# First projection block of a two-layer encoder step: the norm weight loaded as one row and spread by TensorE, the first weight unit and the first norm in halves, both full token tiles loaded ahead of it, low parts made in the order in which TensorE reads them

## The chip, the cores and the metric

The kernel runs on one core of one Trainium2 chip. The metric is the device time of one execution in microseconds (us), of which a run gives several; the median counts. The engines are TensorE (PE in the profile; its weight loads are PEld), VectorE (DVE), ScalarE (ACT), GpSimd (POOL) and SyncE (SP), which here only issues transfers.

## What is computed

One inference step for 256 new frames and 64 continued frames through two layers, each an attention sub-layer and a mixture of 16 experts. The change touches only the beginning of layer 0: the first norm and the first block of columns of the projection.

```python
def rms_norm(x, gain):
    xf = x.astype(jnp.float32)
    y = xf * lax.rsqrt(jnp.mean(xf * xf, axis=-1, keepdims=True) + EPS)
    return (y * gain.astype(jnp.float32)).astype(x.dtype)
...
        hp = rms_norm(xp, norm_mix[i])
        hs = rms_norm(xs, norm_mix[i])
...
    q, k, v = jnp.split(h @ w_in, 3, axis=-1)     # layer 0: w_in is 1024 x 3072, float32
```

`x` has 1024 columns, and everything is float32.

## The kernel before

**Tiles and units.** The tokens are three tiles of 128 rows (`x[:, t, :]`, t = 0, 1, 2); the third has 64 real rows. The weights of a projection come in units of 1 MB: 512 rows by 512 columns, kept as 128 partitions of four blocks of 512 numbers (`w_raw`, six slots). A block `b` of 512 output columns needs two units, `half` 0 (input rows 0 to 511) and `half` 1 (rows 512 to 1023). Layer 0 has six such blocks (q, q, k, k, v, v), then attention, the output projection and the experts, and layer 1 follows with the same stages.

**Split products.** To keep float32 accuracy, every weight and every activation of a projection is split in two: a high part that ScalarE makes by a copy to the rounded type (`split_hi` L769 for weights into `w_hi`, `h_high` L797 for activations into `hT_hi`), and a low part, the difference, that VectorE makes (`split_lo` L1680 into `w_lo`, `h_low` L1702 into `hT_lo`). TensorE then does three matmuls of 128x512 per 128 input rows, high by high, high by low and low by high (L1114 to L1116). For tile 2 the low rows lie in the unused partitions of `hT_hi`, and two matmuls are enough (L1169, L1170). One `half` of a block is therefore 12 + 12 + 8 = 32 matmuls.

**The first block.** SyncE issues, in this order, `x` tile 0, the identity, the norm weight spread over 128 partitions by the transfer (512 KB), unit 0, `x` tile 1, unit 1, `x` tile 2, the other constants, and further units as their slots become free. For each tile ScalarE squares and sums (L791), GpSimd makes the reciprocal root (L601, L602), VectorE multiplies by it and by the norm weight (L1692), TensorE transposes eight blocks of 128x128 into the memory banks of `ps` (L1141), ScalarE and VectorE make high and low parts. TensorE transposes tile 0 first, does the first six matmuls of tile 0, transposes tile 1, does the next twelve, transposes tile 2, and goes on; from there the work of `half` 1, and of all blocks behind it, follows without transposes of `h`.

**Order.** Each engine has its instructions in program order, written out by hand, and waits on counting semaphores: `lo_ready` counts units whose low part is there, `lo0` the low parts of `hT`, `h_ready0` the normed tiles, `hi_ready` the high parts of units. In ScalarE's order the high part of unit 0 stands ahead of the copies of tile 0's transposes, and the high part of unit 1 ahead of the square of tile 2. In VectorE's order the low part of unit 0 stands ahead of tile 0's low parts and of tile 1's norm.

Slots of weights are released by TensorE's progress (`units_used`), so SyncE issues most later transfers when TensorE has finished with an earlier unit.

Elsewhere in the kernel `stay_busy(bank, n)` (L1118 to L1122) issues n matmuls of 128x256 on constants whose result nobody reads.

## Time and profile before

| what | value |
|---|---|
| time of the kernel before, median of 3 runs | 958.04 us |
| the three runs | 958.04, 959.68, 950.64 us |
| the profiled execution: its own time | 956.53 us |
| its span (first to last instruction) | 954.7 us |
| TensorE busy, share of the span | 96% |
| VectorE, ScalarE, GpSimd busy | 42%, 32%, 17% |
| mean granted clock of TensorE | 0.987 |

The span is what the profile's rows are counted in; 1.8 us of the execution's time lie around it. A row of the timeline has start and duration in us, the engine, the line, the operation with output and inputs, how many instructions it stands for, and in square brackets how long the engine had been idle and what ended that. A full-precision matmul (L1122, or L1206 of the changed kernel) shows as two records in the trace, a split product's matmul and a transpose as one.

### The profile page before, as it was taken

The numbers are of one execution on the slowest core, as the hardware profiler recorded it, in microseconds if no ns is written. First come the engines' busy times: TensorE is split into PE (matmuls) and PEld (weight loads), VectorE is DVE, ScalarE is ACT, GpSimd is POOL, SyncE is SP. The second block draws the span as 40 slices with busy tenths as digits, with TensorE's granted clock in tenths as the row PEclk, the third lists the DMA queues.
The fourth block names the chain that finished last, engine by engine and source line by source line (L and its number), as shares of the span: only waits on it lengthen the run. The fifth ranks groups of instructions, "written<-read, shape, count | busy, mean of one in ns | idle before, by whom it ended". The sixth has DMA issues, their size and how long they took to land.

```text
span 954.7 us, 11823 instructions
## 1 busy us (share of the span) xinstructions
PE 915.4 (96%) x4596; PEld 559.7 (59%) x4596; DVE 398.2 (42%) x836; ACT 309.2 (32%) x631; POOL 159.0 (17%) x220
## 2 busy tenths in 40 slices
PE   3999999999999999999899999999999999999997
PEld 2878766787443444443478777776886344444443
DVE  4666467525121223223748554464434122222123
ACT  4545458714110111112435445464332111111110
POOL 2524323310000000000321344441010000000000
PEclk9999989999999999999999999999899999999999
DMA  9844642279799999999434463454867999999994
GB/s 309 264 132 138 214 135 79 71 275 397 299 422 423 420 423 422 417 410 420 144 97 132 160 186 101 140 138 157 331 264 322 402 423 421 423 421 422 421 422 178
DMA packets 56779, 271.56 MB, mean 284 GB/s; under 512 B 5840, under 2 KB 6080, under 8 KB 32144
## 3 DMA queue, kind: packets, MB, share of 16 engines
q1 hardware_dynamic: 47824, 242.66, 64.3%
q0 software_dynamic: 8896, 28.09, 9.2%
q8 instruction: 40, 0.66, 0.3%
q14 instruction: 19, 0.16, 0.0%
HBM read 260.96 MB, written 9.77 MB: 284 GB/s over the span
## 4 chain that ended last, share of the span: by engine, by line
PE 89%; DVE 4%; DMA 3%; ACT 2%; issue 1%; POOL 1%; SPq 0%; ACTq 0%; DVEq 0%
PE ps L1557 22%; PE ps L1575 12%; PE ps L1114 8%; PE ps L1116 7%; PE ps L1115 7%; PE ps L1589 2%; PE ps L1169 2%; PE ps L1170 2%; PE ps L1590 2%; PE ps L1334 2%; PE ps L1338 2%; PE ps L1254 2%; PE ps L1531 1%; DMA w_raw<-in_diff_w_in 1%; DMA w_raw<-in_moe_w_up 1%; PE ps L1251 1%
## 5 line engine op out<-in xcount | busy, mean ns | idle before, releaser
L1557 PE MATMUL ps<-w_extra,xT 128*64 128x512 f32 x512 | 162.6, 594 | 2.1 <-DMA w_raw<-in_moe_w_up 2.1
L1557 PE MATMUL ps<-w_raw,xT 128*64 128x512 f32 x320 | 142.0, 593 | 0.0
L1114 PE MATMUL ps<-w_hi,hT_hi 128*128 128x512 f32 x224 | 94.4, 421 | 5.9 <-DVE hT_lo L1702 5.6
L1680 DVE TENSOR_TENSOR w_lo<-w_raw,w_hi 128x2048 fp32r<-128x2048 f32 x33 | 75.1, 2287 | 54.8 <-ACT w_hi L769 54.8
L1115 PE MATMUL ps<-w_lo,hT_hi 128*128 128x512 f32 x224 | 89.0, 398 | 0.0
L1116 PE MATMUL ps<-w_hi,hT_lo 128*128 128x512 f32 x224 | 89.0, 397 | 0.0
L1557 PE MATMUL ps<-w_more,xT 128*64 128x512 f32 x192 | 85.1, 594 | 0.0
L1557 PEld LDWEIGHTS ps<-w_raw,xT 128*64 128x64 f32 x320 | 43.2, 137 | 71.2 <-issue 71.2
L1575 PE MATMUL ps<-w_extra,hidT 128*64 128x512 f32 x240 | 82.8, 596 | 0.0
L1557 PEld LDWEIGHTS ps<-w_extra,xT 128*64 128x64 f32 x512 | 50.1, 137 | 51.9 <-issue 51.8
L1575 PE MATMUL ps<-w_raw,hidT 128*64 128x512 f32 x168 | 75.7, 597 | 0.0
L769 ACT ACTIVATE w_hi<-w_raw 128x2048 fp32r<-128x2048 f32 x33 | 62.4, 1908 | 26.0 <-PE ps L1170 18.7
L2068 DVE TENSOR_TENSOR x<-x,ps 128x1024 f32<-128x1024 f32 (+1 forms) x48 | 56.9, 1216 | 11.3 <-PE ps L1590 11.3
L2088 DVE SCALAR_TENSOR_TENSOR hid<-hid,slot_gate,ps 128x512 f32<-128x512 f32 x16 | 12.0, 747 | 107.6 <-PE ps L1557 107.6
L1114 PEld LDWEIGHTS ps<-w_hi,hT_hi 128*128 128x128 f32 x224 | 42.5, 190 | 18.1 <-DVE w_lo L1680 4.8
L2062 DVE TENSOR_TENSOR y_lo<-ps,y_hi 128x512 fp32r<-128x512 f32 x32 | 22.1, 692 | 70.1 <-ACT y_hi L1057 70.0
L744 POOL DMA_INDIRECT x_slots<-h_rows,slot_row x7 | 6.9, 986 | 260.8 <-DVE slot_row L2044 179.7
L1116 PEld LDWEIGHTS ps<-w_hi,hT_lo 128*128 128x128 f32 x224 | 42.4, 189 | 10.3
L1115 PEld LDWEIGHTS ps<-w_lo,hT_hi 128*128 128x128 f32 x224 | 42.6, 190 | 7.7
L839 ACT ACTIVATE probs<-probs,stat 128x128 f32<-128x128 f32 (+2 forms) x80 | 40.8, 512 | 14.3 <-DVE stat L1779 12.6
L1575 PE MATMUL ps<-w_more,hidT 128*64 128x512 f32 x104 | 43.6, 597 | 0.0
L1057 ACT ACTIVATE y_hi<-ps 128x512 fp32r<-128x512 f32 x32 | 19.1, 597 | 74.1 <-PE ps L1575 74.1
(303 smaller groups left out, 1630.0 us busy)
## 6 DMA issues: line engine op xcount, KB each, us to landing
w_extra<-in_moe_w_up SPq DMA_DIRECT2D x35, 1024.0 KB, 17.0
w_extra<-in_moe_w_down SPq DMA_DIRECT2D x30, 1024.0 KB, 17.8
w_extra<-in_moe_w_gate SPq DMA_DIRECT2D x29, 1024.0 KB, 16.7
w_raw<-in_moe_w_gate SPq DMA_DIRECT2D x25, 1024.0 KB, 16.4
w_raw<-in_moe_w_down SPq DMA_DIRECT2D x21, 1024.0 KB, 15.8
w_raw<-in_fox_w_in SPq DMA_DIRECT2D x16, 1024.0 KB, 5.4
w_raw<-in_moe_w_up SPq DMA_DIRECT2D x15, 1024.0 KB, 13.2
w_more<-in_moe_w_up SPq DMA_DIRECT2D x14, 1024.0 KB, 20.5
```

Of the source, the lines that this page charges most:

```text
L769: A_(w_hi[:, U.hslot, :], w_raw[:, U.slot, :], ACT.Copy).then_inc(hi_ready, 1)
L839: ins = A_(s, s, ACT.Exp, bias=nmx[:, j % 3, c:c + 1], scale=scale, accum_out=sm[:, j % 3, c:c + 1])
L1057: A_(y_hi[:, c * F:(c + 1) * F], ps[:, 3 + c, :], ACT.Copy).then_inc(L["y_hi"], 1)
L1114: mm(out, a_hi, b_hi, start=start, stop=False)
L1115: mm(out, a_hi, b_lo, start=False, stop=False)
L1116: return mm(out, a_lo, b_hi, start=False, stop=stop)
L1169: mm(acc(b, t), a_hi[:, kb, ts], hi[:, k, :], start=(kb == 0), stop=False)
L1557: ins = mm(ps[j * CAP:(j + 1) * CAP, bank, :], xT[:, kb, j * CAP:(j + 1) * CAP], buffer(U.slot)[:, k * F:(k + 1) * F], start=(kb == 0), st ...
L1575: ins = mm(ps[j * CAP:(j + 1) * CAP, 3 + c, :], hidT[:, fb, j * CAP:(j + 1) * CAP], buffer(U.slot)[:, k * D + c * F:k * D + (c + 1) * F], ...
L1680: v.tensor_tensor(w_lo[:, U.slot, :], w_raw[:, U.slot, :], w_hi[:, U.hslot, :].bitcast(F32), ALU.subtract).then_inc(lo_ready, 1)
L2062: v.tensor_tensor(y_lo[:, cs], ps[:, 3 + c, :], y_hi[:, cs].bitcast(F32), ALU.subtract).then_inc(L["y_lo"], 1)
L2068: v.tensor_tensor(x[0:n, t, :], x[0:n, t, :], ps[0:n, BACK[t]:BACK[t] + 2, :].rearrange("p b n -> p (b n)"), ALU.add).then_inc(L["x_added" ...
```

## The change

Only the start of layer 0 is written anew.

- The norm weight is loaded as one row of 4 KB in place of 512 KB. VectorE sets a row of 128 ones, and TensorE multiplies it with the row, in two matmuls of 512 columns, into banks 6 and 7 of `ps`. The three norms of layer 0 read the weight there.
- SyncE's order is now `x` tile 0, the row, the identity, `x` tile 1, unit 0 as two transfers of 512 KB, `x` tile 2, unit 1, the other constants, further units.
- Unit 0 is split into high and low parts in two halves of 1024 columns, each with a count of its own. The norm of tile 0 is made in two halves of 512 columns, and its transposes start behind the first.
- The low parts come in the order tile 0 first half, tile 1 first half, tile 0 second half, tile 1 second half, tile 2, and TensorE waits for each by that order. The transposes of tiles 0 to 2 go to other banks.
- TensorE gets two matmuls of 128x256 on `x` ahead of tile 0's transposes and four behind them (`warm`), whose results nobody reads.
- The counts of the semaphores follow (`split_parts`), and two loads of layer 1 share a semaphore. Layer 1 keeps its order.

```diff
@@ -430,6 +432,16 @@
                 return dst_lo[:, ks, t * P:(t + 1) * P]
             return dst_hi[:, ks, 2 * P + DEC:3 * P]
 
+        def split_parts(U):
+
+            return U.p + 2
+
+        def low_order(l):
+
+            return (0, 2, 1, 3, 4, 5) if l == 0 else (0, 1, 2, 3, 4, 5)
+
+        IN_BANKS = [(0, 3, 1, 4, 2, 5), (0, 1, 2, 3, 4, 5)]
+
         def in_kind(b):
             return "qqkkvv"[b]
 
...
@@ -500,8 +512,9 @@
                 sp.dma_start(x[0:ROWS[t], t, :], token_rows(x_p, x_s, t)).then_inc(x_loaded[t], 16)
 
             load_x(0)
+            sp.dma_start(gain[0:1, 0, :], A["norm_mix"][0:1, :]).then_inc(ident_loaded, 16)
             sp.dma_start(ident, A["c_consts"][:, C_ID:C_ID + P]).then_inc(ident_loaded, 16)
-            sp.dma_start(gain[:, 0, :], A["norm_mix"][0, :].partition_broadcast(P)).then_inc(gain_loaded[0][0], 16)
+            load_x(1)
 
             def load_unit(U, src, shape=None):
                 if U.free:
...
@@ -515,9 +528,14 @@
                     if l == 0 and b == 1:
                         sp.dma_start(cst[:, C_ID + P:], A["c_consts"][:, C_ID + P:]).then_inc(const_loaded, 16)
                     for half in range(2):
-                        load_unit(IN[l][2 * b + half], src_proj(W_IN[l], b, half), F)
-                        if l == 0 and b == 0:
-                            load_x(1 + half)
+                        if l == 0 and b == 0 and half == 0:
+                            U, src = IN[0][0], src_proj(W_IN[0], 0, 0)
+                            rows = buffer(U.slot).rearrange("p (k n) -> p k n", n=F)
+                            sp.dma_start(rows[:, 0:2, :], src[:, 0:2, :]).then_inc(first_loaded, 16)
+                            sp.dma_start(rows[:, 2:4, :], src[:, 2:4, :]).then_inc(raw_ready[U.slot], 16)
+                            load_x(2)
+                        else:
+                            load_unit(IN[l][2 * b + half], src_proj(W_IN[l], b, half), F)
 
             def load_experts(l):
                 attention_over = ranks_over = False
...
@@ -784,30 +802,35 @@
                     if l == 0:
                         act.wait_ge(x_loaded[t], 16)
                         if t == 2:
-                            act.wait_ge(x_padded, 1)
+                            act.wait_ge(x_padded, 2)
                     else:
 
                         act.wait_ge(L["x_added"], 3 * MPAIRS - 3 + t + 1)
                     A_(h[:, t, :], x[:, t, :], ACT.Square, accum_out=ss[:, t:t + 1]).then_inc(L["sq0"], 1)
 
-                def h_high(t):
-                    for i in (2 * t, 2 * t + 1):
+                def h_high(t, halves=(0, 1)):
+                    for i in (2 * t + half for half in halves):
                         act.wait_ge(L["tr0"], B["tr0"] + i + 1)
-                        dst, src = hi_part(hT_hi, i)
+                        dst, src = hi_part(hT_hi, i, IN_BANKS[l][i])
                         A_(dst, src, ACT.Copy).then_inc(L["hi0"], 1)
 
                 square_in(0)
+                square_in(1)
                 if l == 0:
-                    split_hi(IN[l][0])
-                    h_high(0)
-                square_in(1)
-                if l == 1:
+                    U, c = IN[0][0], UNIT // 2
+                    act.wait_ge(first_loaded, 16)
+                    A_(w_hi[:, U.hslot, 0:c], w_raw[:, U.slot, 0:c], ACT.Copy).then_inc(hi_ready, 1)
+                    h_high(0, (0,))
+                    act.wait_ge(raw_ready[U.slot], U.arrivals)
+                    A_(w_hi[:, U.hslot, c:UNIT], w_raw[:, U.slot, c:UNIT], ACT.Copy).then_inc(hi_ready, 1)
+                    square_in(2)
+                    h_high(0, (1,))
+                    h_high(1)
+                    split_hi(IN[0][1])
+                else:
                     square_in(2)
                     h_high(0)
-                if l == 0:
-                    split_hi(IN[l][1])
-                    square_in(2)
-                h_high(1)
+                    h_high(1)
                 h_high(2)
                 if l == 0:
                     split_hi(IN[l][2])
...
@@ -1147,18 +1170,19 @@
 
                 for half in range(2):
                     U = units[2 * b + half]
-                    pe.wait_ge(lo_ready, U.p + 1)
+                    pe.wait_ge(lo_ready, split_parts(U) if U.p else 1)
                     hi, lo = unit_parts(U, F)
                     for t in range(TILES):
                         if b == 0 and half == 0 and t == 2 and B["tr0"]:
                             last_transposes(2)
                         if b == 0:
-                            pe.wait_ge(L[low], B[low] + 2 * t + half + 1)
+                            pe.wait_ge(L[low], B[low] + low_order(l).index(2 * t + half) + 1)
                         if half == 0 and free is not None:
                             free(b, t)
                         for k in range(4):
                             if b == 0 and half == 0 and t < 2 and k == 2 and not B["tr0"]:
                                 last_transposes(t + 1)
+                                pe.wait_ge(lo_ready, split_parts(U))
                             kb = 4 * half + k
                             ts = slice(t * P, (t + 1) * P)
                             if t < 2:
...
@@ -1176,13 +1200,31 @@
                     if half == 0 and between is not None:
                         between()
 
-            pe.wait_ge(ident_loaded, 16)
+            def warm(n):
+
+                for _ in range(n):
+                    mm(ps[:, 5, 0:256], ident, x[:, 0, 0:256], start=True, stop=True)
+
+            pe.wait_ge(x_padded, 1)
+            pe.wait_ge(ident_loaded, 32)
+            for c in range(2):
+                mm(ps[:, 6 + c, :], ones_row[0:1, :], gain[0:1, 0, c * F:(c + 1) * F], start=True, stop=True).then_inc(gain_spread, 1)
+            pe.wait_ge(x_loaded[0], 16)
             for l in range(2):
                 B = BEFORE[l]
-                transposes(B, h, "h_ready0", "tr0", tiles=(0,) if l == 0 else (0, 1))
+                if l == 0:
+                    warm(2)
+                    pe.wait_ge(L["h_ready0"], 1)
+                    for k in range(4):
+                        ins = tr(ps[:, 0, k * P:(k + 1) * P], h[:, 0, k * P:(k + 1) * P], ident)
+                    ins.then_inc(L["tr0"], 1)
+                    transposes(B, h, "h_ready0", "tr0", counts=(2, 3, 4), only=(1,), banks=IN_BANKS[0])
+                    warm(4)
+                else:
+                    transposes(B, h, "h_ready0", "tr0", tiles=(0, 1))
 
                 def last_in(t):
-                    transposes(B, h, "h_ready0", "tr0", tiles=(t,))
+                    transposes(B, h, "h_ready0", "tr0", counts=(2, 3, 4) if l == 0 else (1, 2, 3), tiles=(t,), banks=IN_BANKS[l])
 
                 def forget_logits():
                     pe.wait_ge(fox["wf_lo"], 1)
...
@@ -1691,31 +1733,48 @@
                     dve.wait_ge(L[rstd_name], B[rstd_name] + t + 1)
                     v.scalar_tensor_tensor(dst[:, t, :], x[:, t, :], rstd[:, t:t + 1], gain[:, which, :], ALU.mult, ALU.mult).then_inc(L[done], 1)
 
+            v.memset(ones_row[:, :], 1.0).then_inc(x_padded, 1)
             v.memset(x[DEC:P, 2, :], 0.0).then_inc(x_padded, 1)
             for l in range(2):
                 B = BEFORE[l]
-                dve.wait_ge(gain_loaded[l][0], 16)
-                def h_low(t):
-                    for i in (2 * t, 2 * t + 1):
+                if l == 1:
+                    dve.wait_ge(gain_loaded[l][0], 16)
+                def h_low(t, halves=(0, 1)):
+                    for i in (2 * t + half for half in halves):
                         dve.wait_ge(L["hi0"], B["hi0"] + i + 1)
-                        hi, src = hi_part(hT_hi, i)
+                        hi, src = hi_part(hT_hi, i, IN_BANKS[l][i])
                         v.tensor_tensor(lo_part(hT_hi, hT_lo, i), src, hi.bitcast(F32), ALU.subtract).then_inc(L["lo0"], 1)
 
-                norm(B, "rstd0", 0, l, h, "h_ready0", tiles=(0,))
                 if l == 0:
-                    split_lo(IN[l][0])
+                    U, c = IN[0][0], UNIT // 2
+                    spread = ps[:, 6:8, :].rearrange("p b n -> p (b n)")
+
+                    def first_norms(t, cols=slice(0, D)):
+                        dve.wait_ge(L["rstd0"], t + 1)
+                        dve.wait_ge(gain_spread, 1 if cols.stop == F else 2)
+                        return v.scalar_tensor_tensor(h[:, t, cols], x[:, t, cols], rstd[:, t:t + 1], spread[:, cols], ALU.mult, ALU.mult)
+
+                    first_norms(0, slice(0, F)).then_inc(L["h_ready0"], 1)
+                    first_norms(0, slice(F, D)).then_inc(L["h_ready0"], 1)
+                    dve.wait_ge(hi_ready, 1)
+                    v.tensor_tensor(w_lo[:, U.slot, 0:c], w_raw[:, U.slot, 0:c], w_hi[:, U.hslot, 0:c].bitcast(F32), ALU.subtract).then_inc(lo_ready, 1)
+                    h_low(0, (0,))
+                    first_norms(1).then_inc(L["h_ready0"], 1)
+                    dve.wait_ge(hi_ready, 2)
+                    v.tensor_tensor(w_lo[:, U.slot, c:UNIT], w_raw[:, U.slot, c:UNIT], w_hi[:, U.hslot, c:UNIT].bitcast(F32), ALU.subtract).then_inc(lo_ready, 1)
+                    h_low(1, (0,))
+                    first_norms(2).then_inc(L["h_ready0"], 1)
+                    h_low(0, (1,))
+                    h_low(1, (1,))
+                    split_lo_half(IN[0][1], 0)
+                    h_low(2)
+                    split_lo_half(IN[0][1], 1)
+                else:
+                    norm(B, "rstd0", 0, l, h, "h_ready0", tiles=(0, 1))
                     h_low(0)
-                norm(B, "rstd0", 0, l, h, "h_ready0", tiles=(1,))
-                if l == 1:
-                    h_low(0)
-                if l == 1:
                     norm(B, "rstd0", 0, l, h, "h_ready0", tiles=(2,))
                     h_low(1)
-                else:
-                    split_lo(IN[l][1])
-                    norm(B, "rstd0", 0, l, h, "h_ready0", tiles=(2,))
-                    h_low(1)
-                h_low(2)
+                    h_low(2)
                 if l == 0:
                     split_lo(IN[l][2])
                     split_lo(IN[l][3])
```

Two places in the order of the instructions show what moves. First TensorE (PE), from the start of the program to its seventh matmul of the projection. `h` is the normed input, `cst` holds the identity, `ps` are the banks of the matmuls' results. Before:

```order
L1141 MATMUL ps<-cst,h 128x128 [waits h_ready0,ident_loaded]
L1141 MATMUL ps<-cst,h 128x128 x3
L1141 MATMUL ps<-cst,h 128x128 [waits h_ready0]
L1141 MATMUL ps<-cst,h 128x128 x3
L1114 MATMUL ps<-w_hi,hT_hi 128x512 [waits lo0,lo_ready]
L1115 MATMUL ps<-w_lo,hT_hi 128x512
L1116 MATMUL ps<-w_hi,hT_lo 128x512
```

Now, where the lines have moved (L1164 and L1219 are transposes, L1137 to L1139 the split product):

```order
L1211 MATMUL ps<-gain,ones_row 128x512 [waits ident_loaded,x_padded]
L1211 MATMUL ps<-gain,ones_row 128x512
L1206 MATMUL ps<-x,cst 128x256 [waits x_loaded0]
L1206 MATMUL ps<-x,cst 128x256
L1219 MATMUL ps<-cst,h 128x128 [waits h_ready0]
L1219 MATMUL ps<-cst,h 128x128 x3
L1164 MATMUL ps<-cst,h 128x128 [waits h_ready0]
L1164 MATMUL ps<-cst,h 128x128 x3
L1206 MATMUL ps<-x,cst 128x256 x4
L1137 MATMUL ps<-w_hi,hT_hi 128x512 [waits lo0,lo_ready]
```

Two matmuls that spread the norm weight and six that only occupy the engine now stand ahead of the first matmul of the projection.

Second VectorE (DVE), from its start to the low parts of unit 1. Before:

```order
L1694 MEMSET x 64x1024
L1692 SCALAR_TENSOR_TENSOR h<-x,stat,gain 128x1024 [waits rstd0,gain_loaded00]
L1680 TENSOR_TENSOR w_lo<-w_raw,w_hi 128x2048 [waits hi_ready]
L1702 TENSOR_TENSOR hT_lo<-ps,hT_hi 128x4x128 [waits hi0] x2
L1692 SCALAR_TENSOR_TENSOR h<-x,stat,gain 128x1024 [waits rstd0]
L1680 TENSOR_TENSOR w_lo<-w_raw,w_hi 128x2048 [waits hi_ready]
L1692 SCALAR_TENSOR_TENSOR h<-x,stat,gain 128x1024 [waits rstd0]
L1702 TENSOR_TENSOR hT_lo<-ps,hT_hi 128x4x128 [waits hi0] x2
```

Now (L1755 is the norm, L1746 the low part of `hT`, L1760, L1764 and L1727 half a unit's low part):

```order
L1755 SCALAR_TENSOR_TENSOR h<-x,stat,ps 128x512 [waits gain_spread,rstd0] x2
L1760 TENSOR_TENSOR w_lo<-w_raw,w_hi 128x1024 [waits hi_ready]
L1746 TENSOR_TENSOR hT_lo<-ps,hT_hi 128x4x128 [waits hi0]
L1755 SCALAR_TENSOR_TENSOR h<-x,stat,ps 128x1024 [waits gain_spread,rstd0]
L1764 TENSOR_TENSOR w_lo<-w_raw,w_hi 128x1024 [waits hi_ready]
L1746 TENSOR_TENSOR hT_lo<-ps,hT_hi 128x4x128 [waits hi0]
L1755 SCALAR_TENSOR_TENSOR h<-x,stat,ps 128x1024 [waits gain_spread,rstd0]
L1746 TENSOR_TENSOR hT_lo<-ps,hT_hi 128x4x128 [waits hi0] x2
L1727 TENSOR_TENSOR w_lo<-w_raw,w_hi 128x1024 [waits hi_ready]
```

Half of unit 0 and one low part of tile 0 are now ahead of tile 1's norm, and unit 1, which stood between the norms of tiles 1 and 2, is behind the third norm and the low parts of tiles 0 and 1.

## Rows read from the trace of the kernel before

**Rows 1.** The page: busy time of each engine, share of the span, records.

```profile
PE 915.4 (96%) x4596; PEld 559.7 (59%) x4596; DVE 398.2 (42%) x836; ACT 309.2 (32%) x631; POOL 159.0 (17%) x220
```

**Rows 2.** What PE waited for, whole span: us in total, times, longest.

```profile
PE ps L1141 <- DVE h L1692: 12.5, 2, 9.5
PE ps L1114 <- DVE hT_lo L1702: 5.6, 2, 4.4
```

**Rows 3.** Timeline, 0 to 23 us, all engines (columns as in the section on the profile).

```profile
4.25 1.06 ACT L791 ACTIVATE h<-x 128x1024 f32<-128x1024 f32 x1 [2.23 <-DMA x<-in_x_prompt]
...
5.85 0.56 POOL L602 TENSOR_TENSOR stat<-stat,neghalf 128x1 f32<-128x1 f32 x1
8.10 1.28 DVE L1692 SCALAR_TENSOR_TENSOR h<-x,stat,gain 128x1024 f32<-128x1024 f32 x1 [6.18 <-DMA gain<-in_norm_mix]
...
9.53 1.94 PE L1141 MATMUL ps<-cst,h 128*128 128x128 f32 x8 [9.53 <-DVE h L1692]
10.92 1.91 ACT L769 ACTIVATE w_hi<-w_raw 128x2048 fp32r<-128x2048 f32 x1 [5.52 <-DMA w_raw<-in_diff_w_in]
12.74 1.07 ACT L797 ACTIVATE hT_hi<-ps 128x512 fp32r<-128x512 f32 x2
12.86 2.29 DVE L1680 TENSOR_TENSOR w_lo<-w_raw,w_hi 128x2048 fp32r<-128x2048 f32 x1 [3.48 <-ACT w_hi L769]
...
15.07 1.28 DVE L1702 TENSOR_TENSOR hT_lo<-ps,hT_hi 128x512 fp32r<-128x512 f32 x2
...
15.90 0.76 PE L1114 MATMUL ps<-w_hi,hT_hi 128*128 128x512 f32 x1 [4.43 <-DVE hT_lo L1702]
```

**Rows 4.** Timeline of PE, 20 to 30 us.

```profile
20.73 0.63 PE L1115 MATMUL ps<-w_lo,hT_hi 128*128 128x512 f32 x1
21.16 0.45 PE L1116 MATMUL ps<-w_hi,hT_lo 128*128 128x512 f32 x1
...
23.46 0.50 PE L1114 MATMUL ps<-w_hi,hT_hi 128*128 128x512 f32 x1 [1.16 <-DVE hT_lo L1702]
...
24.97 1.04 PE L1141 MATMUL ps<-cst,h 128*128 128x128 f32 x8
...
29.11 0.39 PE L1114 MATMUL ps<-w_hi,hT_hi 128*128 128x512 f32 x1
29.34 0.40 PE L1115 MATMUL ps<-w_lo,hT_hi 128*128 128x512 f32 x1
```

**Rows 5.** The three loads of `x`, issued at 0.74, 2.60 and 3.64 us: time to landing.

```profile
DMA to landing us min/median/max: 3.5/9.6/14.1
```

**Rows 6.** Units 0 and 1: issues at 2.12 and 3.15 us, time to landing.

```profile
DMA to landing us min/median/max: 8.8/11.1/13.4
```

**Rows 7.** The spread norm weight, issue 1.65 us: time to landing.

```profile
DMA to landing us min/median/max: 6.4/6.4/6.4
```

**Rows 8.** The identity, issue 1.19 us: time to landing.

```profile
DMA to landing us min/median/max: 3.2/3.2/3.2
```

**Rows 9.** Chain of waits, 120 to 123 us: three full-precision matmuls of 128x256.

```profile
120.94 1.30 PE ps L1122 x6
```

**Rows 10.** PE's busy time by stretch: us, PE busy, granted clock, DMA share, GB/s.

```profile
core 0: us, PE busy (x), PEclk, DMA share, GB/s
...
36.30:100.00 63.70, 63.70 (x292) 1.00 0.51 170
```

**Rows 11.** The same view, the two longest stretches at the low granted clock.

```profile
127.00:133.90 6.90, 6.90 (x27) 0.51 0.04 14
...
666.40:676.60 10.20, 8.79 (x47) 0.50 0.57 210
```

**Rows 12.** Timeline of DVE: low parts of units 2, 3 and 4.

```profile
28.27 6.70 DVE L1680 TENSOR_TENSOR w_lo<-w_raw,w_hi 128x2048 fp32r<-128x2048 f32 x3 [1.38 <-ACT w_hi L769]
```

**Rows 13.** The page: DVE on 128x512 with `ps` as input.

```profile
L2088 DVE SCALAR_TENSOR_TENSOR hid<-hid,slot_gate,ps 128x512 f32<-128x512 f32 x16 | 12.0, 747 | 107.6 <-PE ps L1557 107.6
```

**Rows 14.** What SP's queue waited for, whole span.

```profile
SPq L511 <- PE ps L1170: 201.4, 22, 30.0
```

24 lines of the change are left out of this document (13 added, 11 removed).

## The prediction

> **What bounds the kernel now.** I began with the page's busy times: PE is busy for 915.4 us, 96% of the span [rows 1], so time can only come from PE's waits or from a slower clock. Then I read what PE waited for. Two entries stand out, 12.5 us for `h` and 5.6 us for `hT_lo` [rows 2]. Of these 9.5 + 4.4 + 1.2 us lie in the first 24 us, where the change is made, so I read the timeline there.
>
> The reader should see one chain [rows 3]. `x` tile 0 is there at 4.25 us, its square and root are done at 6.4, but the norm of tile 0 starts at 8.10, released by the transfer of the spread norm weight, which took 6.4 us from its issue at 1.65 [rows 7]. PE transposes tile 0 from 9.53 to 11.47. Unit 0 lands at 10.9 (issue 2.12 + 8.8 [rows 6]), its high part ends at 12.8, its low part at 15.1, and only then come the low parts of `hT`. PE's first matmul of the projection is at 15.90.
>
> The second thing to see is the pace of PE. At 20.73 and 21.16 two matmuls of 512 columns follow each other by 0.43 us, at 29.11 and 29.34 by 0.23 us [rows 4]. That is 1.2 GHz at first and near 2.4 GHz later. The rise came at about 21.2, 5.3 us after PE had begun near-unbroken work. The granted clock does not record the first stretch, so the spacing is what tells it. At 23.46 PE had waited 1.16 us more for tile 1's low part.
>
> `half` 1 of block 0 starts at 29.11 [rows 4]. From there PE is busy without a gap: 63.70 of 63.70 us between 36.3 and 100 [rows 10]. So 29.1 us is the number to beat, and what it gains is what the kernel gains if nothing behind it is late.
>
> **The change, part by part.** I follow the new order and ask when PE reaches the same matmul. I assume that the clock rises 5.4 us after PE begins to be busy, as it did before.
>
> *Loads.* SyncE now issues the row at 1.2 and the identity at 1.65 us. At the identity's 3.2 us to landing [rows 8] both are there at 4.85. Tile 1 takes the place, in bytes, of the spread weight (512 KB each): 8.1 us. The first half of unit 0 then ends 0.5 MB before the point that unit 0 reached at 10.9, so between 8.1 and 10.9: 9.5; the second half at 10.9. Tile 2 follows at about 12. It landed at 17.7 before (3.64 + 14.1 [rows 5]), but behind unit 1. Unit 1 was there at 16.5 (3.15 + 13.4 [rows 6]); 0.25 MB less stands ahead of it now, so 15.5.
>
> *Spreading the norm weight.* Three full-precision matmuls of 256 columns took 1.30 us at the high clock [rows 9], 0.43 each. One of 512 columns is 0.87 at the high and 1.7 at the low clock. Two of them run from 4.85 to 8.3 at the low clock, with the halves visible at 6.9 and 8.6. If one row instead of 128 as input made them cheaper the lower bound is the 0.43 of a plain matmul at this clock [rows 4], and the norm would gain up to 2.5 us. I take 1.7, from the row that is the same kind of operation.
>
> *Norm of tile 0.* 512 columns with an input in `ps` took 0.75 us [rows 13]. First half 6.9 to 7.6, second 8.6 to 9.4. The whole norm ended at 9.4 before. So the row in place of the spread transfer gains nothing for the end of this norm. It gains the 0.5 MB of transfer ahead of tile 1 and unit 0, and it gives PE work from 4.85 on.
>
> *The matmuls whose results nobody reads.* Two take 1.7 us at the low clock, 8.3 to 10.0. The first transposes wait behind them though their input was there at 7.7. Eight transposes cost 1.94 at the low clock [rows 3] and 1.04 with the last one's tail, some 0.9 in spacing, at the high one [rows 4]. With the rise at 10.3 they end at 11.2, and four more of the idle matmuls at 12.8 (at the low clock it would be 15.3).
>
> *First half of unit 0.* ScalarE's 1.91 us for a unit halves to 0.96, VectorE's 2.29 to 1.15 [rows 3]. High part 9.5 to 10.5, low part to 11.7, then tile 0's first low part of 0.68 (two took 1.28 [rows 3]) to 12.4. PE is ready at 12.8, so the first real matmul moves from 15.9 to 12.8.
>
> *The rest of `half` 0.* Six matmuls at 0.23 end at 14.2. Tile 1's norm (VectorE, 12.5 to 13.7) is done, eight transposes end at 15.1. The second half of unit 0 has its low part at 15.0. Six matmuls to 16.5; tile 1's first low part is ready at 16.3. Six more to 17.9; tile 2's norm is ready at 17.5. Transposes to 18.8, six matmuls to 20.2. For tile 2's low part VectorE first does the norm of tile 2, two low parts of 0.65 and half of unit 1: 20.4. Eight matmuls to 22.3. Unit 1 is complete on VectorE at 22.0. PE starts `half` 1 at 22.3 instead of 29.1: 6.8 us.
>
> *What is queued behind.* Four of PE's waits end within 0.3 us of PE's own arrival, so VectorE has become as late as PE, and each hand-over between engines costs some of it. I take off 0.5 us for them, from gaps such as 9.38 to 9.53 between norm and transposes [rows 3]: 6.3 us. Units 2, 3 and 4 had their low parts from 28.27 to 34.97 before [rows 12], and PE needed the first at 36.3. Now unit 1 leaves VectorE at 22.0, unit 2's low part ends at about 24.5, and PE needs it at 29.8, so nothing is late there. The later transfers are released by PE's own matmuls; SP waited 201.4 us for these [rows 14], so they move with it. The merged semaphore of layer 1 and the added memset I cost at nothing: both lie beside PE's work.
>
> The sum against the profiled execution: 956.5 - 6.3 = 950.2 us. That execution was 1.5 us under the median of the three runs (958.04), from which the same sum gives 951.7. I predict 951.0, between them.
>
> *Where the page on TensorE speaks against it.* The rows show a rise at 21.2 in a stretch from 15.90 that held twelve matmuls and eight transposes [rows 3, 4]; they don't show which of these it was owed to. The Trainium skill, "TensorE: Matmul & The Clock Gate", Part 4, says that transposes do not count as PE-busy in the same way. By that rule the idle matmuls around the transposes are what is needed, and the rise may come later than I put it. No row here shows whether a matmul with a single input row counts.
>
> **The rivals.**
>
> *The clock does not rise early.* If PE's single-row matmuls, idle matmuls and transposes do not bring the rise, it comes only some 5 us after the projection's own matmuls begin. The warm-up then costs its low price, first real matmul at 15.3, the rise near 18 to 21, and `half` 1 starts at 26.2 to 27.5: a gain of 1.6 to 2.9 us, 954 to 955 us. For it: eight transposes at 9.53 to 11.47 did not bring the clock up by 15.9. Against it: PE was idle for 4.4 us behind these, and now it is not.
>
> *A transfer is as late as before.* ScalarE's square of tile 2 stands ahead of three copies that tile 1 and the second half of tile 0 need. If tile 2 lands at 17.7 as before, ScalarE stands until then, tile 1 starts some 4 us later, and `half` 1 starts at 27.0: 2.1 us gained, 954.4. For it: the load took 14.1 us before, and its issue was the seventh then as now. Against it: 1.5 MB more stood ahead of it.
>
> *Slower: more time at the low clock further down.* The granted clock was 0.50 to 0.51 in stretches of 6.9 us at 127 and of 10.2 us at 666, in attention and behind it, where PE waits often [rows 11]. All of attention now falls 6 us earlier against whatever decides when the clock is lowered. Each microsecond of PE's work at the low clock costs half a microsecond. From 12.6 us more of it the start's gain is gone. With two more stretches such as the one at 666 (8.79 us busy each) 8.8 us are lost: 956.5 - 6.3 + 8.8 = 959 us or more. Against it: PE's work there is the same. The three runs of before lie 9 us apart without any change, so such shifts exist in both directions.
>
> *The gain is absorbed later.* If some stage were bound by something that does not move with PE, 956 to 958 us. The rows speak against it, since transfers are released by PE.
>
> **How the numbers follow.** The forecast, a gain of 5 to 7.5 us, gets 0.62, with its own range of 946 to 954. The clock that rises late 0.20, the late transfer 0.10, more low clock further down 0.05, absorption 0.03. The scatter of the runs adds to each. The range is 944.5 to 957.5: below by 6.8 us off the fastest run of before (950.6 gives 943.8), above by the rivals' 955 with the scatter of about 2.5. A measurement of this kernel can tell about 1% from no change, 9.6 us. My forecast of 0.7% lies inside that. Faster by over 1% needs the full gain and a lucky share of low clock: 0.22. Slower by over 1%: 0.04. Within 1%: 0.74.
>
> **What would show it.** Right, if in the new profile PE's first L1211 starts near 4.9, matmuls of 512 columns stand 0.23 apart from the first L1137 on, that L1137 starts near 12.8 and `half` 1 near 22.5 to 23, and from there PE has no gap until attention. The first step is wrong if L1211 takes much less than 1.7 us each. The clock is wrong if the first matmuls of the projection are 0.43 apart. The order is wrong if PE waits over 1 us for L1746 of tile 1 or for unit 1. The forecast fails as a whole if the shift at `half` 1 is there and the end has not moved by as much.

## The result, and the profile after

| | kernel before | changed kernel |
|---|---|---|
| median of 20 runs each | 957.42 us (950.64 to 963.66) | 951.54 us (945.73 to 957.60) |
| ratio | | 0.9942, 95% interval 0.9919 to 0.9966 |
| profiled execution: span, mean granted clock | 954.7 us, 0.987 | 945.1 us, 0.990 |
| `half` 1 of block 0 begins | 29.11 us [rows 4] | 22.77 us |

The change is worth 0.6%, 5.5 us by the ratio; 951.0 was forecast. The two profiled executions differ by 9.6 us, and that difference has to be taken apart before it is believed. Line numbers below are those of the changed kernel: `L1137` to `L1139` are the matmuls of tiles 0 and 1, `L1193` and `L1194` those of tile 2, `L1164` and `L1219` transposes, `L1211` spreads the weight, `L1206` is the idle matmul, `L1746` a low part of `hT`, `L1755` a norm.

The page's busy times first (they answer [rows 1]), then what PE waited for up to 140 us, in all, times, longest (answers [rows 2]):

```profile
PE 916.5 (97%) x4612; PEld 559.5 (59%) x4612; DVE 398.1 (42%) x840; ACT 309.4 (33%) x632; POOL 156.7 (17%) x220
```

```profile
PE ps L1211 <- DMA cst<-in_c_consts: 4.5, 1, 4.5
PE ps L1345 <- DVE probs L1858: 2.3, 2, 1.2
PE ps L1330 <- DVE low_rows L1808: 0.3, 1, 0.3
```

PE is 1.1 us busier than before. The idle matmuls and the two that spread the weight add 7.8 us, so all other work took 6.7 us less: about 2.7 us of that is the 5.3 us of work at the low clock at the start of the projection, which now runs at the high one, and 3.4 us lie further down (below). The waits of 9.5, 4.4 and 1.2 us are gone, and one of 4.5 us for the first load is all that is left of the start. Lines 1345 and 1330 belong to attention.

The timeline of the start, ScalarE, VectorE and TensorE (answers [rows 3]):

```profile
4.50 3.75 PE L1211 MATMUL ps<-gain,ones_row 1*128 1x512 f32 x4 [4.50 <-DMA cst<-in_c_consts]
6.66 0.75 DVE L1755 SCALAR_TENSOR_TENSOR h<-x,stat,ps 128x512 f32<-128x512 f32 x1 [4.50 <-PE ps L1211]
...
8.18 2.08 PE L1206 MATMUL ps<-x,cst 128*128 128x256 f32 x4
8.36 0.75 DVE L1755 SCALAR_TENSOR_TENSOR h<-x,stat,ps 128x512 f32<-128x512 f32 x1 [0.95 <-PE ps L1211]
...
9.47 1.06 ACT L822 ACTIVATE w_hi<-w_raw 128x1024 fp32r<-128x1024 f32 x1 [0.21 <-DMA w_raw<-in_diff_w_in]
10.05 1.06 PE L1219 MATMUL ps<-cst,h 128*128 128x128 f32 x4
...
10.90 1.06 PE L1164 MATMUL ps<-cst,h 128*128 128x128 f32 x4
...
11.75 1.97 PE L1206 MATMUL ps<-x,cst 128*128 128x256 f32 x8
11.77 0.69 DVE L1746 TENSOR_TENSOR hT_lo<-ps,hT_hi 128x512 fp32r<-128x512 f32 x1
...
13.37 0.58 PE L1137 MATMUL ps<-w_hi,hT_hi 128*128 128x512 f32 x1
...
14.02 0.39 PE L1139 MATMUL ps<-w_hi,hT_lo 128*128 128x512 f32 x1
14.24 0.40 PE L1137 MATMUL ps<-w_hi,hT_hi 128*128 128x512 f32 x1
14.48 0.39 PE L1138 MATMUL ps<-w_lo,hT_hi 128*128 128x512 f32 x1
```

See two things. PE has no bracket behind 4.50: it goes from the spreading to idle matmuls, transposes, idle matmuls and the first real matmul at 13.37 (15.90 before). And the matmuls from 14.02 on stand 0.23 apart, the high clock, where before they stood 0.43 apart until 21.2 [rows 4]. The clock rose about 11.9 us, among the idle matmuls: eight records in 1.97 us, where four took 2.08 at 8.18.

PE at the start of `half` 1, from the timeline (answers [rows 4]), and then its busy time by stretch (answers [rows 10, 11]):

```profile
22.54 0.39 PE L1194 MATMUL ps<-w_lo,hT_hi 128*128 128x512 f32 x1
22.77 0.40 PE L1137 MATMUL ps<-w_hi,hT_hi 128*128 128x512 f32 x1
```

```profile
core 0: us, PE busy (x), PEclk, DMA share, GB/s
22.77:94.50 71.73, 71.73 (x327) 1.00 0.62 203
114.30:117.70 3.40, 3.40 (x10) 0.50 0.93 273
...
657.00:667.20 10.20, 8.68 (x46) 0.50 0.59 215
```

`half` 1 begins 6.34 us earlier and PE is busy without a gap from there. One group of eight transposes of the projection stage starts at 100.82 us in the chain of waits of before, and the same group at 94.48 here, again 6.34. Up to there the gain passes on unchanged. The other 3.3 us of the 9.6 are time at the low clock: a stretch of 6.9 us at 127 before [rows 11] is one of 3.4 at 114 now, and one of 3.4 us at 219 is gone. That is 6.9 us less at half pace, worth 3.4. The stretch of 10.2 us at 666 stands at 657 with its length unchanged. The two places in the trace of before:

```profile
core 0: us, PE busy (x), PEclk, DMA share, GB/s
...
121.00:134.00 13.00, 11.60 (x52) 0.74 0.47 164
216.00:224.00 8.00, 7.47 (x44) 0.79 1.02 423
```

The same stretches in the changed kernel:

```profile
core 0: us, PE busy (x), PEclk, DMA share, GB/s
...
121.00:134.00 13.00, 12.67 (x82) 1.00 0.21 71
216.00:224.00 8.00, 7.79 (x46) 1.00 1.02 425
```

Whether these 3.3 us are the change's or the execution's is what the last runs below ask.

### The profile page after: what moved, and what is told of

It is laid out like the page before. It is cut to its first block, busy times and chain, and to the rows that moved or that the text cites. A ratio compares the mean times of both kernels' runs of the same rounds, so it can differ in the third digit from the quotient of the medians.

```text
span 945.1 us, 11864 instructions
## 1 busy us (share of the span) xinstructions
PE 916.5 (97%) x4612; PEld 559.5 (59%) x4612; DVE 398.1 (42%) x840; ACT 309.4 (33%) x632; POOL 156.7 (17%) x220
## 4 chain that ended last, share of the span: by engine, by line
PE 91%; DVE 4%; ACT 2%; DMA 2%; issue 1%; POOL 0%; SPq 0%; ACTq 0%; DVEq 0%
PE ps L1599 22%; PE ps L1617 12%; PE ps L1137 8%; PE ps L1139 7%; PE ps L1138 7%; PE ps L1631 2%; PE ps L1193 2%; PE ps L1194 2%; PE ps L1632 2%; PE ps L1376 2%; PE ps L1380 2%; PE ps L1573 2%; PE ps L1296 1%; PE ps L1164 1%; DMA w_raw<-in_moe_w_up 1%; PE ps L1293 1%
## 5 line engine op out<-in xcount | busy, mean ns | idle before, releaser
L1137 PE MATMUL ps<-w_hi,hT_hi 128*128 128x512 f32 x224 | 93.6, 418 | 0.3 <-DVE gate L1950 0.3
L1722 DVE TENSOR_TENSOR w_lo<-w_raw,w_hi 128x2048 fp32r<-128x2048 f32 x31 | 70.6, 2286 | 51.1 <-ACT w_hi L787 51.1
L1139 PE MATMUL ps<-w_hi,hT_lo 128*128 128x512 f32 x224 | 88.5, 395 | 0.0
L787 ACT ACTIVATE w_hi<-w_raw 128x2048 fp32r<-128x2048 f32 x32 | 60.7, 1909 | 21.2 <-PE ps L1194 14.7
L1137 PEld LDWEIGHTS ps<-w_hi,hT_hi 128*128 128x128 f32 x224 | 42.1, 188 | 11.6 <-issue 1.5
L1139 PEld LDWEIGHTS ps<-w_hi,hT_lo 128*128 128x128 f32 x224 | 42.0, 187 | 10.1
## 6 DMA issues: line engine op xcount, KB each, us to landing
w_raw<-in_moe_w_up SPq DMA_DIRECT2D x15, 1024.0 KB, 12.6
```

What stands on the lines that cost most here:

```text
L787: A_(w_hi[:, U.hslot, :], w_raw[:, U.slot, :], ACT.Copy).then_inc(hi_ready, 1)
L1137: mm(out, a_hi, b_hi, start=start, stop=False)
L1139: return mm(out, a_lo, b_hi, start=False, stop=stop)
L1722: v.tensor_tensor(w_lo[:, U.slot, :], w_raw[:, U.slot, :], w_hi[:, U.hslot, :].bitcast(F32), ALU.subtract).then_inc(lo_ready, 1)
```

## The experiments

Each edit is against the changed kernel unless it says otherwise. `half` 1 is when the first `L1114`/`L1137` matmul of that half begins. Most kernels below ran once, beside one run of the kernel before on the same chip; the total of one run scatters by several us, so the start is read from its profile instead. How far the start itself scatters was measured twice: the changed kernel had `half` 1 at 22.77 and, in its repetition (the last kernel of this section), at 23.83; the kernel before with idle matmuls at 31.53 and, on another chip, at 29.71. Differences at `half` 1 of up to 1.8 us between single profiles are therefore not shown.

| kernel | PE waits, us | first real matmul | `half` 1 | its one run |
|---|---|---|---|---|
| changed kernel | none | 13.37 | 22.77 | |
| no idle matmuls | 1.7 | 12.22 | 23.21 | 954.07 |
| weight spread by the transfer | 1.8, 0.4 | 13.60 | 23.11 | 952.84 |
| both of these | 3.1 | 13.98 | 24.77 | 955.82 |
| tile 1 loaded behind unit 0 | none | 13.64 | 23.70 | 955.17 |
| unit 0 whole | 3.2 | 17.61 | 29.57 | 955.28 |
| old order of the parts | 5.5 | 13.17 | 30.85 | 956.41 |
| order alone | 7.8 | 18.24 | 28.92 | 958.42 |
| before with idle matmuls | 2.0, 3.0 | 15.79 | 31.53 | 953.80 |

The waits are those behind the first instruction, for a low part of `hT` (in the third row the 1.8 is for the norm). The kernel before took 958.40 beside rows two to four and the last, and 953.95 beside the others.

### The idle matmuls and the row

```diff
-                    warm(2)
-                    warm(4)
```

> The changed kernel without the six idle matmuls on x. The changed kernel starts half 1 of block 0 at 22.8 us, its clock rises at about 11.8, while the last four idle matmuls run. Theory (the idle matmuls bring the clock up, the single-row matmuls alone do not): PE reaches the first matmul of the projection earlier, near 12.5, but at the low clock (512 columns 0.43 us apart), the rise comes only between 16 and 18, half 1 starts at 24.5 to 25.5. Rival (the gain is order and halves, the idle matmuls are ballast): rise no later than 12.5, half 1 at 22.3 or earlier.

The first matmul came earlier, but behind a wait and at the low clock; the rise came at 15.8:

```profile
12.22 0.77 PE L1137 MATMUL ps<-w_hi,hT_hi 128*128 128x512 f32 x1 [1.75 <-DVE hT_lo L1744]
12.79 0.63 PE L1138 MATMUL ps<-w_lo,hT_hi 128*128 128x512 f32 x1
13.21 0.63 PE L1139 MATMUL ps<-w_hi,hT_lo 128*128 128x512 f32 x1
```

The low clock is there as the theory has it, but `half` 1 is only 0.4 us later, not 2. From the first matmul to `half` 1 it takes 10.99 us in place of 9.40: the low clock costs 1.6 us, in the first six matmuls (2.70 us in place of 1.58) and in part of the transposes behind them. But the first matmul starts 1.15 us earlier, because PE doesn't stand behind its own idle matmuls. They cost nearly what they bring. Theory and rival both missed.

```diff
-            sp.dma_start(gain[0:1, 0, :], A["norm_mix"][0:1, :]).then_inc(ident_loaded, 16)
+            sp.dma_start(gain[:, 0, :], A["norm_mix"][0, :].partition_broadcast(P)).then_inc(gain_spread, 16)
...
-                mm(ps[:, 6 + c, :], ones_row[0:1, :], gain[0:1, 0, c * F:(c + 1) * F], start=True, stop=True).then_inc(gain_spread, 1)
```

> The changed kernel with the norm weight spread by the transfer of 512 KB again, issued behind the identity as before; all else as changed, the six idle matmuls too. Theory (the row is worth its 0.5 MB ahead of tile 1 and unit 0, about 1.3 us): tile 1 lands near 9.5, the first half of unit 0 near 10.8, first matmul of the projection near 13.8, half 1 at 23.8 to 24.8. Rival (the spread by PE ends at the same time as the transfer did, so the row gains nothing): half 1 at 22.8 within 0.3.

23.11, at the edge of what the rival says: alone the row is worth 0.3 us at `half` 1, less than the scatter. Unit 0's second half landed at 13.1 instead of 11.8, which is what the 512 KB cost, and PE did not need it before.

> As the run with the spread by the transfer, and without the six idle matmuls: order and halves alone. Theory: PE's only work ahead of the projection is eight transposes, the clock stays low until 17 to 20, half 1 at 25.5 to 27.5. Rival (order and halves are the whole gain): half 1 at 24 or earlier.

24.77, 2.0 us later, between theory and rival. The first matmul is 0.6 us later and the low clock costs 1.4 us behind it. Each of the two parts covers for the other: the row keeps the loads short, so that PE starts early, and the idle matmuls bring the clock up. Together they are worth about 2 of the 6.3 us, hardly more than the scatter; in these single profiles one of them alone brings nearly all of it.

### The halves and the order

```diff
-                            sp.dma_start(rows[:, 0:2, :], src[:, 0:2, :]).then_inc(first_loaded, 16)
-                            sp.dma_start(rows[:, 2:4, :], src[:, 2:4, :]).then_inc(raw_ready[U.slot], 16)
+                            sp.dma_start(rows, src).then_inc(raw_ready[U.slot], 16)
...
-                    A_(w_hi[:, U.hslot, 0:c], w_raw[:, U.slot, 0:c], ACT.Copy).then_inc(hi_ready, 1)
...
-                    A_(w_hi[:, U.hslot, c:UNIT], w_raw[:, U.slot, c:UNIT], ACT.Copy).then_inc(hi_ready, 1)
+                    A_(w_hi[:, U.hslot, :], w_raw[:, U.slot, :], ACT.Copy).then_inc(hi_ready, 2)
```

VectorE's low part of unit 0 is made whole in the same way.

> The changed kernel with unit 0 loaded and split whole; row, idle matmuls and order as changed. Theory: the high part runs from 10.9 to 12.8, the low part to 15.1, the first matmul of the projection is near 15.9 instead of 13.4, half 1 starts 1.5 to 2.5 us later than the changed kernel's 22.8, at 24.3 to 25.3. Rival (the halves only move time into later waits): 22.8 to 23.3.

Much more than either. The timeline (ScalarE, VectorE, PE), and the clock of the stretch from 16.4:

```profile
12.56 1.91 ACT L821 ACTIVATE w_hi<-w_raw 128x2048 fp32r<-128x2048 f32 x1 [3.55 <-DMA w_raw<-in_diff_w_in]
14.38 0.58 ACT L814 ACTIVATE hT_hi<-ps 128x512 fp32r<-128x512 f32 x1
14.57 2.29 DVE L1757 TENSOR_TENSOR w_lo<-w_raw,w_hi 128x2048 fp32r<-128x2048 f32 x1 [5.30 <-ACT w_hi L821]
...
17.61 0.76 PE L1134 MATMUL ps<-w_hi,hT_hi 128*128 128x512 f32 x1 [3.21 <-DVE hT_lo L1743]
...
20.31 1.91 PE L1161 MATMUL ps<-cst,h 128*128 128x128 f32 x8
```

```profile
16.40:23.20 6.80, 5.59 (x17) 0.51 1.07 372
```

The whole unit is there at 12.6, the first half was at 9.4, and the copies of the transposes stand behind it. So the first matmul comes 4.2 us later. PE waits 3.2 us for it, and the clock, which had been up since 13.1, is lowered again for 6.8 us. With that `half` 1 is 6.8 us later.

```diff
-            return (0, 2, 1, 3, 4, 5) if l == 0 else (0, 1, 2, 3, 4, 5)
+            return (0, 1, 2, 3, 4, 5)
...
-                    square_in(2)
                     h_high(0, (1,))
-                    h_high(1)
                     split_hi(IN[0][1])
+                    square_in(2)
+                    h_high(1)
```

VectorE's order goes back in the same way, both halves of unit 1 ahead of tile 2's norm and tile 1's low parts.

> The changed kernel with the old order of the parts on ScalarE and VectorE: both low parts of tile 0 together, then unit 1, then tile 2's norm, then tile 1's low parts. Row, halves, loads and idle matmuls stay as changed. Theory (before, the wait for unit 1's transfer stood ahead of tile 1's low parts; to put them ahead of it is the largest part of the gain): PE waits over 3 us for tile 1's low part, which comes near 22, and half 1 starts at 26.5 to 28.5. Rival (the gain is the earlier start of the projection and the clock, and the order among the low parts is worth 1 us or less): half 1 at 22.8 to 24.

The wait that the theory asks for is there, and larger. ScalarE, VectorE and PE in the timeline:

```profile
15.92 1.91 ACT L787 ACTIVATE w_hi<-w_raw 128x2048 fp32r<-128x2048 f32 x1 [2.15 <-DMA w_raw<-in_diff_w_in]
...
17.87 2.36 DVE L1727 TENSOR_TENSOR w_lo<-w_raw,w_hi 128x1024 fp32r<-128x1024 f32 x2 [1.92 <-ACT w_hi L787]
...
18.78 1.06 ACT L815 ACTIVATE hT_hi<-ps 128x512 fp32r<-128x512 f32 x2
20.67 1.28 DVE L1755 SCALAR_TENSOR_TENSOR h<-x,stat,ps 128x1024 f32<-128x1024 f32 x1 [0.44 <-POOL stat L620]
21.86 1.28 DVE L1746 TENSOR_TENSOR hT_lo<-ps,hT_hi 128x512 fp32r<-128x512 f32 x2
```

```profile
22.60 0.80 PE L1137 MATMUL ps<-w_hi,hT_hi 128*128 128x512 f32 x1 [5.53 <-DVE hT_lo L1746]
```

ScalarE stands at unit 1 until it lands at 15.9, and tile 1's copies and low parts stand behind it. PE, long past tile 1's transposes, waits 5.5 us, and is at the low clock from 21.4 to 28.2 (granted clock 0.50). With everything else of the change in place, `half` 1 is 8.1 us later than in the changed kernel and 1.7 later than before. This is the wait of the kernel before as well: there ScalarE stood at unit 1 until 16.56, and tile 1's low part was ready only at 23.46 [rows 4], against 16.90 in the changed kernel.

Of the 6.8 and the 8.1 us, some 2.8 us each are the low clock behind the wait (5.6 us of work at half pace). A wait of 3.4 us in a later profile brought no such stretch. What does not hang on it is the rest, about 4.0 us for the halves and 5.3 us for the order.

> Only the new order of loads and of high and low parts: the norm weight is spread by the transfer of 512 KB, unit 0 is loaded and split whole, no idle matmuls. With unit 0 in halves the same kernel started half 1 at 24.77. Theory (halving unit 0 brings the first matmul forward by about 1.2 us of VectorE's and 1 us of ScalarE's time, but PE then waits elsewhere): first matmul at 15 to 16.5, half 1 at 25.5 to 27. Rival (the halves are needless once the order is right): half 1 at 24.8 within 0.3.

(The weight spread by the transfer, unit 0 whole, no idle matmuls; the new order and loads stay.) 28.92, later than both theory and rival: the order alone gives nothing. Unit 0 now lands at 13.2, since 512 KB of tile 1 stand ahead of it beside the spread weight, and PE waits 7.8 us for the first low part. Halves and order are not two gains to be added. The order without halves makes unit 0 late, the halves without the order leave the wait for unit 1.

```diff
             load_x(0)
...
-            load_x(1)
...
+                            load_x(1)
...
-                square_in(1)
+                if l == 1:
+                    square_in(1)
...
-                    h_high(0, (0,))
...
+                    h_high(0, (0,))
+                    square_in(1)
```

(Tile 1 is loaded behind unit 0. ScalarE makes both high parts of unit 0, then the first copy of tile 0, then the square of tile 1.)

> The changed kernel with tile 1 loaded behind unit 0 instead of ahead of it; ScalarE squares tile 1 behind the high parts of unit 0 and the first copy of tile 0. Theory (the low parts of unit 0 come at least 1 us earlier, tile 1's norm some 2 us later; PE cannot use the first since its idle matmuls end at 13.4): first matmul at 13.4, half 1 at 22.8 to 23.7. Rival (tile 1 ahead of unit 0 is what lets the new order work): half 1 at 24.5 or later.

23.70, as the theory expected, but 0.9 us is within the scatter of the start: that tile 1 goes first is not shown to matter.

### The high clock by itself

The kernel before with six idle matmuls ahead of tile 0's transposes and eight behind:

```diff
+            pe.wait_ge(x_loaded[0], 16)
+            warm(6)
...
+                if l == 0:
+                    warm(8)
```

> The kernel before with idle matmuls alone: six of 128x256 on x ahead of tile 0's transposes and eight behind them, so that PE is busy from 4.4 us to the projection. Theory (the clock is one part of three): the first matmul of the projection stays at 15.9, all matmuls are 0.23 apart, but PE now waits for tile 1's low part, so half 1 starts at 27 to 28.2 instead of 29.1. Rival (the clock is nearly the whole gain): half 1 at 24 or earlier.

The clock rose at 8.7 and nothing was gained: `half` 1 begins at 31.53, 2.4 us later than before. What PE waited for up to 36 us:

```profile
PE ps L1114 <- DVE hT_lo L1711: 5.0, 2, 3.0
```

TensorE at twice the pace only reached the same two low parts of `hT` sooner. Tile 1's was there at 23.03 (23.46 before), and while PE waited the clock was lowered again, 0.50 granted from 22.4 to 29.2. Theory and rival were both wrong, and with them my picture of the low clock as a cost of its own. Yet its one run was 4.6 us faster than before, with a later start. I come back to that.

### More at the start

Four idle matmuls on constants from 1.31 us, one instead of two and three instead of four behind:

> The changed kernel with four idle matmuls of 128x256 from about 1.5 us on, on a tile that VectorE sets to 0.5, ahead of the two that spread the norm weight; behind these one idle matmul instead of two and, behind tile 0's transposes, three instead of four. Theory (in the changed kernel the last idle matmul ends 0.9 us after VectorE was ready at 12.46, and the clock rose only at 11.8): the clock rises at 8 to 9.5, PE reaches the first matmul of the projection when VectorE is ready, near 12.5, and half 1 starts at 21.8 to 22.4 instead of 22.8; time 0.5 to 1 us under the changed kernel's 951.5. Rival (VectorE and the transfers set the pace from there on, so an earlier PE only waits): half 1 at 22.6 to 22.9.

```profile
1.31 3.78 PE L1210 MATMUL ps<-hid 128*128 128x256 f32 x8 [1.31 <-DVE hid L1739]
5.02 3.77 PE L1213 MATMUL ps<-gain,ones_row 1*128 1x512 f32 x4
8.73 1.22 PE L1206 MATMUL ps<-x,cst 128*128 128x256 f32 x2
9.74 1.06 PE L1221 MATMUL ps<-cst,h 128*128 128x128 f32 x4
10.59 1.06 PE L1164 MATMUL ps<-cst,h 128*128 128x128 f32 x4
11.45 2.59 PE L1206 MATMUL ps<-x,cst 128*128 128x256 f32 x6
13.65 0.61 PE L1137 MATMUL ps<-w_hi,hT_hi 128*128 128x512 f32 x1
```

PE is busy from 1.31 and still at the low clock after 11.45 (six records in 2.59 us, where eight took 1.97 before). `half` 1 begins at 23.10, so the theory fell; the rival's 22.9 is within the scatter. The median of 6 runs was 949.33 against 959.25, ratio 0.9894 (0.9860 to 0.9929).

Fourteen more idle matmuls, `warm(18)` for `warm(4)`, a plain delay of PE:

> The changed kernel with fourteen further idle matmuls behind tile 0's transposes, 6.0 us at the high clock: a plain delay of PE at the start. Theory (the start's time passes to the end one for one): half 1 near 28.8, the ratio to the kernel before 1.000 within its interval, near 957.5 us. Rival (a later stage absorbs a shift of the start, and the gain came otherwise): ratio 0.994 to 0.996, 951 to 954 us.

`half` 1 begins at 29.96, 7.2 us later than in the changed kernel and 0.85 later than before. The time was 953.76 (12 runs) against 959.25, ratio 0.9951 (0.9925 to 0.9977). By the start alone it should have been 1.001. The theory's 1.000 lies outside the interval and the rival's 0.994 to 0.996 was met, but at equal clock (below) it is the theory that holds.

### Is the gain the start's, or the clock's further down?

Two kernels on one chip: the kernel before with idle matmuls again, now with twelve runs, and the changed kernel again.

> The kernel before with 6 idle matmuls ahead and 8 behind tile 0's transposes, as in the single look above, now timed in rounds. Its half 1 begins 2.4 us later than before's and 8.8 later than that of the changed kernel. Theory (what the start gains or loses at half 1 passes on one for one): 0.25% slower than before, ratio 1.0025, and 0.9% slower than the changed kernel on the same chip. Rival (the shape of the start also decides how long TensorE stands at the low clock in the attention stage, some 6.8 us of it): ratio 0.993 to 0.997 with a later half 1, and at most 0.4% behind the changed kernel.

> The changed kernel again, on the same chip and beside the run above. Theory (the start passes on one for one, the rest of the time is the same): half 1 at 22.8, ratio to before 0.993 to 0.994, that is 6.3 us. Rival (part of the gain is less time at the low clock in the attention stage, as in the first profile): ratio 0.989 to 0.992, with no more than 3.4 us at the low clock between 100 and 225 us in this profile too.

| kernel | runs | median us | ratio to before (95%) | mean granted clock | us at clock 0.986 | `half` 1 |
|---|---|---|---|---|---|---|
| before, beside rows 4, 5 | 17 | 959.25 | | 0.9851 | 958.0 | |
| before, beside rows 6, 7 | 17 | 958.14 | | 0.9854 | 958.6 | |
| changed kernel | 20 | 951.54 | 0.9942 (0.9919 to 0.9966) | 0.9862 | 951.4 | 22.77 |
| idle matmuls from 1.31 us | 6 | 949.33 | 0.9894 (0.9860 to 0.9929) | 0.9885 | 951.1 | 23.10 |
| `warm(18)` | 12 | 953.76 | 0.9951 (0.9925 to 0.9977) | 0.9898 | 957.2 | 29.96 |
| before with idle matmuls | 12 | 960.00 | 0.9996 (0.9967 to 1.0026) | 0.9850 | 958.5 | 29.71 |
| changed kernel again | 6 | 952.22 | 0.9898 (0.9866 to 0.9931) | 0.9860 | 951.5 | 23.83 |

On one chip the last two rows differ by 7.8 us in the median, with 5.9 us between their starts. The kernel before with idle matmuls came out at 0.9996. Its start was other than expected: `half` 1 at 29.71, 0.6 us later than before and not 2.4. Theory (1.0025) and rival (0.993 to 0.997) both lie near the edges of its interval; against the changed kernel it is 0.8% slower in the median, where the theory said 0.9% and the rival at most 0.4%. Its single run of 953.80 was as fast as the fastest of these 12. For the changed kernel 0.9898 is in the rival's range, with the theory's 0.993 at the edge of the interval, but the profile refuted the rival's condition: that execution had 17 us at the low clock between 100 and 225, where the rival allowed 3.4. So 0.9898 is no proof of another cause.

The sixth column says more. Every run lists its mean granted clock, and within one kernel the time follows it: the three fastest runs of the changed kernel (945.7 to 946.9 us) had 0.990 to 0.992, the three slowest (956.7 to 957.6) 0.980. I fitted a time for each row and one common slope to all 90 runs of the table (the 20 runs of before beside row 3 are listed without their clocks, so row 3 is compared with the two other rows of before). The column at clock 0.986 gives the fitted times. The slope is 8.3 us for 0.01 of clock and the rest scatters by 1.2 us. The figures in brackets are half widths of 95% intervals. At equal clock the changed kernel is 6.9 us (0.7) faster than before, and 7.1 (1.1) in its repetition; the start says 6.3. `warm(18)` is 0.9 (0.9) faster, where the start says 0.85 slower, and it is 5.8 us behind the changed kernel, with 7.2 us between their starts; before with idle matmuls 0.1 (0.9) faster, the start says 0.6 slower. The early idle matmuls are 7.0 (1.1) faster, the start says 6.0. All are what the start says, give or take its own scatter of 1 to 2 us. So the changed kernel's gain is the start's as far as this can tell. Its mean clock is 0.001 (0.002) above before's, no difference that shows, and the 3.3 us between the first two profiles are of a size that executions of one kernel differ by. What this does not settle is whether a small part of the 5.5 to 7 us is a higher mean clock: 0.001 of clock is 0.8 us.

What stays open: `warm(18)` ran at a mean clock 0.0047 (plus or minus 0.0021) above before's, some 3.9 us, and the early idle matmuls 0.0034 (0.0021), 2.8 us. Their profiles show no stretch at the low clock between 100 and 225. Why more idle work in the first 20 us should do that wasn't found: fourteen idle matmuls in the kernel before did not (0.9850).

## Why the prediction was right

| step | predicted | measured |
|---|---|---|
| row and identity there | 4.85 | 4.50 |
| norm halves of tile 0 begin | 6.9, 8.6 | 6.66, 8.36 |
| first idle matmuls end | 10.0 | 10.05 |
| clock rises | 10.3 | 11.9 |
| halves of unit 0 there | 9.5, 10.9 | 9.4, 11.8 |
| tile 0's first low part ready | 12.4 | 12.46 |
| first real matmul | 12.8 | 13.37 |
| unit 1 there | 15.5 | 15.5 |
| tile 1's first low part ready | 16.3 | 16.90 |
| `half` 1 with 0.5 for hand-overs | 22.8 | 22.77 |

*The sum* held: 6.3 us forecast, 6.34 in the first pair of profiles. The time taken for a single-row matmul, 1.7 us from the full-precision row [rows 9], was right: the halves of the norm begin 1.70 us apart. Two terms were off and nearly cancelled. The clock rose 7.4 us after PE became busy, not 5.4, so the first matmul was 0.6 us late; this used up the 0.5 us taken off for hand-overs, of which no other is seen, since PE never waited. That they cancel to 0.03 us is luck, and so is the closeness itself: in the repetition `half` 1 began at 23.83, since the first load landed 0.6 us later and the clock rose at 13.4. Unit 0's second half was 0.9 us late, which cost nothing, because VectorE was at tile 1's norm until 13.6. One figure of the forecast does not follow from its text: the fastest run less 6.8 us is 943.8, and the range begins at 944.5.

*The clock.* I weighed a rule of the Trainium skill against my own assumption, that the rise comes 5.4 us after PE begins to be busy. The assumption was wrong as a fixed time. In six profiles PE does the changed kernel's work up to the rise, and the rise came 6.7 to 9.3 us after its start (7.4 in the first). The first 3.7 us of this are the two single-row matmuls. Without them, in the kernel before with idle matmuls, it came after 4.1 and 4.4 us, and it was 5.3 us before. With four idle matmuls ahead of the single-row ones it took over 10. So the time was longer where single-row matmuls stand at the start. That they are the reason is not shown: with the weight spread by the transfer they are gone, but a wait of 1.8 us takes their place, and the rise came at 12.4, no earlier. No run separates the transposes either. "TensorE: Matmul & The Clock Gate", Part 4, of the Trainium skill says that transposes do not count as PE-busy in the same way; the late rise does not speak against it. The rival built on it, no early rise, did not come. Its price of 3.9 to 5.2 us was too high as far as can be seen: without idle matmuls, which is not quite its condition, the rise came at 15.8, the low clock cost 1.6 us behind the first matmul, and `half` 1 was 0.4 us later.

*What I did not see.* The prediction walks through one timeline with all parts in place, and never asks what each is worth. They do not add: two of them undone singly cost 6.8 and 8.1 us of a gain of 6.3, two others 0.3 and 0.4. The order mattered most, because unit 1's landing had stood ahead of tile 1's low parts. My text named unit 0 and the spread weight as the chain and gave the order no term of its own.

*Absorption* was not seen: the shift is 6.34 us at 94 us still, and the totals at equal clock agree with the start. *More low clock further down* was possible in each execution, but no mean of the changed kernel shows it. *Late transfer of tile 2*: it landed at 13.0 instead of 12, just when ScalarE reached it.

## What to carry to other kernels

When an engine starves at the start of a kernel, write down for each engine what stands ahead of the part that is waited for; here it was a load that landed at 16.5 and that PE itself needed only at 29.1. Halving the first unit and reordering pay only together, and a faster clock pays nothing while the consumer waits for a part that another engine makes. Idle matmuls can cost by their own length nearly what the high clock gives back. Before a difference of under 1% is put down to a stage, compare landmarks along the chain and the mean granted clock of every run; a single profiled pair overstated this gain by half.
